# Projection, attention and state-update kernel: where three bonus-related steps stand, narrower turned rows, and another order of the sample value products

## The reference, cut to what matters

```python
h = rmsnorm(x, norm_mix_g);  p = h @ w_in          # 1024 -> 2560 columns
pa, pb = p[..., :SHIFT_W], p[..., SHIFT_W:]        # group A (RWKV-7) and group B (attention)
# group A: token shift, per-head recurrence, bonus
xm = pa + mu_shift * (pa_prev - pa)                # pa_prev: the row before; for a sample, state_shift
bonus = sum(rh * kh * r_k, axis=-1, keepdims=True) * vh
# group B: sliding window of 128, 8 query heads on 2 kv heads, learned sinks, ALiBi
o = einsum('bkgts,bskd->btkgd', p, vals)           # sample: 128 cached rows + 4 new ones
x = x + concat(o_A, rmsnorm(o_B)) @ w_out
x = x + hier_moe(rmsnorm(x));  y = rmsnorm_final(x)
```

## Time and profile before

| | us |
|---|---|
| median of 3 executions | 1196.08 (1192.57 to 1202.50) |
| the profiled execution | 1196.84 |
| its span | 1195.0 |
| granted TensorE clock, mean of the span | 0.982 |

### The profile page before, as it was taken

How to read it: one execution, slowest core, us unless ns; L and a number is a source line. 1 busy time by engine, 2 the same in 40 slices (tenths; PEclk the granted TensorE clock), 3 DMA queues, 4 the chain that set the end, 5 groups by cost and what they waited for, 6 DMA issues and landing times.

```text
span 1195.0 us, 24875 instructions
## 1 busy us (share of the span) xinstructions
PE 1121.5 (94%) x10856; PEld 784.8 (66%) x10856; DVE 464.3 (39%) x930; ACT 362.8 (30%) x808; POOL 259.8 (22%) x153
## 2 busy tenths in 40 slices
PE   5999999999999978888899999889999999999995
PEld 4666666655566657677654444478778887888774
DVE  3300656537775586676835422441101000111034
ACT  3101645442435255654621311210111111011152
POOL 0000000001100059999910000111202112111102
PEclk9999989999999999989999999989999999999998
DMA  6511100001010130002041661268889889998894
GB/s 202 158 36 36 58 18 19 18 18 40 22 35 22 15 57 4 5 4 57 4 170 52 226 236 71 93 222 307 277 312 322 309 288 321 323 320 296 298 388 172
DMA packets 95689, 174.16 MB, mean 146 GB/s; under 512 B 19988, under 2 KB 41175, under 8 KB 95172
## 3 DMA queue, kind: packets, MB, share of 16 engines
q1 hardware_dynamic: 88372, 151.92, 36.6%
q0 software_dynamic: 7200, 20.57, 6.5%
HBM read 147.45 MB, written 27.75 MB: 147 GB/s over the span
## 4 chain that ended last, share of the span: by engine, by line
PE 85%; DVE 9%; issue 2%; ACT 2%; SPq 0%; DMA 0%; POOLq 0%; POOL 0%; DVEq 0%; ACTq 0%
PE ps L740 23%; PE ps L1446 20%; PE ps L1244 9%; PE ps L1469 9%; PE ps L1475 1%; PE ps L819 1%; PE ps L843 1%; PE ps L832 1%; PE ps L956 1%; PE ps L1422 1%; PE ps L997 1%; PE ps L944 1%; PE ps L1122 1%; ACT arena L1983 1%; PE ps L778 1%
## 5 line engine op out<-in xcount | busy, mean ns | idle before, releaser
L740 PE MATMUL ps<-arena 128*128 128x355 f32 x960 | 302.6, 472 | 1.9 <-issue 1.7
L740 PEld LDWEIGHTS ps<-arena 128*128 128x128 f32 x960 | 182.1, 193 | 109.2 <-issue 13.3
L1446 PEld LDWEIGHTS ps<-arena 128*128 128x128 f32 x2048 | 245.9, 191 | 7.8 <-issue 6.1
L1446 PE MATMUL ps<-arena 128*128 128x128 f32 (+4 forms) x2048 | 248.3, 283 | 0.7 <-ACT arena L1958 0.6
L1244 PE MATMUL ps<-arena 128*128 128x512 f32 x256 | 116.4, 597 | 0.7 <-DVE arena L2346 0.7
L1469 PE MATMUL ps<-arena 128*128 128x512 f32 x256 | 113.3, 595 | 0.7 <-DVE arena L2621 0.7
L1966 ACT ACTIVATE arena<-ps 128x128 f32<-128x128 f32 (+4 forms) x64 | 18.3, 286 | 278.5 <-PE ps L1446 278.5
L2621 DVE TENSOR_TENSOR arena<-arena,ps 128x128 f32<-128x128 f32 (+4 forms) x64 | 19.1, 298 | 212.6 <-ACT arena L1966 212.6
L2806 POOL TENSOR_TENSOR arena<-arena 128x1024 f32<-128x1024 f32 x4 | 11.4, 2853 | 334.5 <-DVE arena L2147 334.5
L1469 PEld LDWEIGHTS ps<-arena 128*128 128x128 f32 x256 | 47.4, 190 | 55.1 <-issue 53.6
L1555 ACT COPY arena<-ps 128x355 f32<-128x355 f32 x60 | 27.1, 452 | 184.8 <-PE ps L740 184.8
(11 more groups left out here) (416 smaller groups left out, 1558.5 us busy)
## 6 DMA issues: line engine op xcount, KB each, us to landing
arena<-in_w_exp_gate SPq DMA_DIRECT2D x16, 2048.0 KB, 10.8
arena<-in_w_exp_up SPq DMA_DIRECT2D x16, 2048.0 KB, 16.4
arena<-in_w_exp_down SPq DMA_DIRECT2D x16, 2048.0 KB, 15.3
arena<-in_w_in SPq DMA_DIRECT2D x16, 512.0 KB, 3.8
arena<-in_x_prompt SPq DMA_DIRECT2D x9, 512.0 KB, 4.4
x_dram<-arena SPq DMA_DIRECT2D x9, 512.0 KB, 3.6
h_dram<-arena SPq DMA_DIRECT2D x8, 512.0 KB, 2.6
out_y_prompt<-arena SPq DMA_DIRECT2D x8, 512.0 KB, 3.7
```

The costliest lines, as they stand in the source:

```text
L740: last = pe.matmul(ps[:, q % 2, 0:m], wr[:, n % 3, k, :], hT[:, k, a:a + m], start=(k == 0), stop=(k == KB - 1))
L1446: last = pe.matmul(ps[:, 3 + f % 2, n * CAP:n * CAP + CAPS[e]], w[a][:, k, f * P:(f + 1) * P], xgT[:, a, k, 0:CAPS[e]], start=(k == 0), st ...
```

## The change

- `hT` loses the gap columns: 1057 columns (`HW`), thirds of 353, 352 and 352 (`G3`). GpSimd's second memset goes. The sample tile is scaled like the others, with one instruction for each four feature blocks. `pT` keeps its gaps, so the third `evict` of each block becomes two copies: 320 prompt columns, and 32 sample columns spread over 8 groups of 4.
- `BONUS_AT` is 74, 86, 99, 117: `bonus`, `smp_turn` and `smp_copy` of the first two pairs stand one half later.
- `a_store(7)` stands before `evict(31)` instead of behind it.
- `s_out` makes both products with new rows first, and then alternates between the kv heads, sample by sample. The number of products stays.

```diff
+HW = 1 + TOK
-G3 = [(0, 355), (355, 355), (710, 355)]
+G3 = [(0, 353), (353, 352), (705, 352)]
...
-        hTf = part(HT0, KB * W)
+        hTf = part(HT0, KB * HW)
...
-        LORA_AT, KK_AT, BONUS_AT = ([2 * q + 1 for q in at] for at in ((31, 37, 43, 50), (33, 39, 45, 52), (36, 42, 49, 58)))
+        LORA_AT, KK_AT = ([2 * q + 1 for q in at] for at in ((31, 37, 43, 50), (33, 39, 45, 52)))
+        BONUS_AT = [74, 86, 99, 117]
...
-            return ap[:, :, 1 + SEQ:W].rearrange("p b (q t) -> p b q t", t=DT + 1)[:, :, :, 1:]
+            return ap[:, :, 1 + SEQ:1 + TOK]
...
-                for kv in range(BKV):
-                    r = slice(kv * HD, (kv + 1) * HD)
-                    out = ps[r, 7, 0:P]
-                    pe.matmul(out, kvnew[:, P + kv * HD:P + (kv + 1) * HD], spk1[:, kv * P:(kv + 1) * P], start=True, stop=False, skip_group_check=True)
-                    for b in range(DB):
-                        view = lambda ap: ap.rearrange("p (g b t) -> p g b t", g=GRP, b=DB)[:, :, b, :]
-                        last = pe.matmul(view(out), vc[:, b, r], view(spk0[:, kv * P:(kv + 1) * P]), start=False, stop=(b == DB - 1), skip_group_check=True)
+                half = [slice(kv * HD, (kv + 1) * HD) for kv in range(BKV)]
+                for kv, r in enumerate(half):
+                    pe.matmul(ps[r, 7, 0:P], kvnew[:, P + kv * HD:P + (kv + 1) * HD], spk1[:, kv * P:(kv + 1) * P], start=True, stop=False, skip_group_check=True)
+                for b in range(DB):
+                    view = lambda ap: ap.rearrange("p (g b t) -> p g b t", g=GRP, b=DB)[:, :, b, :]
+                    for kv, r in enumerate(half):
+                        last = pe.matmul(view(ps[r, 7, 0:P]), vc[:, b, r], view(spk0[:, kv * P:(kv + 1) * P]), start=False, stop=(b == DB - 1), skip_group_check=True)
...
-                act.copy(pT[:, pos, a:a + m], ps[:, q % 2, 0:m]).then_inc(s["p_ok"], 1)
+                if g < 2:
+                    act.copy(pT[:, pos, a:a + m], ps[:, q % 2, 0:m]).then_inc(s["p_ok"], 1)
+                else:
+                    act.copy(pT[:, pos, a:1 + SEQ], ps[:, q % 2, 0:m - NS])
+                    act.copy(sample4(pT[:, pos, 1 + SEQ:W]), by4(ps[:, q % 2, m - NS:m])).then_inc(s["p_ok"], 1)
...
-                if k >= 5 and k % 2:
+                if k >= 5 and k % 2 and k < NU + 3:
                     a_store((k - 5) // 2)
...
+                if UNIT_AT.get(h) == NU + 3:
+                    a_store(NT - 1)
                 if h % 2:
                     evict(h // 2)
...
-                    if t < NT:
-                        dve.tensor_tensor(dst, src, g[:, :, None].to_broadcast([P, 4, n]), ALU.mult).then_inc(s["hT_ok"], 1)
-                    else:
-                        for k in range(4):
-                            last = dve.tensor_scalar(dst[:, k], src[:, k].rearrange("p (b t) -> p b t", t=DT), g[:, k:k + 1], None, ALU.mult)
-                        last.then_inc(s["hT_ok"], 1)
+                    dve.tensor_tensor(dst, src, g[:, :, None].to_broadcast([P, 4, n]), ALU.mult).then_inc(s["hT_ok"], 1)
...
-            pool.memset(hT[:, :, 0:1], 0.0)
-            pool.memset(hT[:, :, 1 + SEQ:W:DT + 1], 0.0).then_inc(s["level_ok"], 1)
+            pool.memset(hT[:, :, 0:1], 0.0).then_inc(s["level_ok"], 1)
```

## The result

The changed kernel took 1187.0 us (median of 13, from 1181.2), the kernel before beside it 1193.3. The ratio is 0.9921, with a 95% interval of 0.9899 to 0.9943; one of the 13 executions of the changed kernel ran slow, at 3545.84 us, and isn't in it. The ratio is not that of the two medians, which stand only 6.3 us apart (0.9947); 0.9921 is 9.4 us. The forecast was 1186.8, within 1%. In a later comparison the changed kernel came to 0.9918 (0.9889 to 0.9947) and 1185.1 us.

The account below looks back on a forecast made before the run. TensorE, busy 94% of the span, was taken to bound the kernel. 2.1 + 6.0 + 1.2 + 0.9 - 0.2 = 10.0 us, from the profiled 1196.84, gave 1186.8 us (chance 0.50); range 1179 to 1194.

Parts of the forecast that it names:

- columns: Projection: thirds lose 2, 3 and 3 columns, so TensorE streams 2560 fewer; 2.1 us gained, bounds 0 and 2.2.
- bonus sums, second pair: Second bonus sum, one half later: its 2.04 us wait for DVE goes and the following step shortens by 0.1 us.
- bonus sums, first pair, with its fall: First bonus sum, one half later: 2.04 us wait and 1.95 us of clock fall go, 0.2 us new wait.
- attention copy: Before the first `lora`: with `a_store(7)` earlier, TensorE's wait goes; 1.2 us gained, bounds 1.0 and 1.3.
- value products: `s_out`: alternating kv heads lets weight loads overlap in the column halves; 0.9 us gained, bounds 0 and 1.3.
- fall behind `s_out`: Rival, more gain: a shorter `s_out` may remove the clock fall behind it, 1.7 us; around 1183 us, chance 0.28.
- split of the last copy: End of the projection: `r_turn` waits for the last third copy, now two instructions; 0.2 us lost.
- start, to `shift_turn`: Start of the projection: 0.07 us saved by five halves of the first third is lost in waiting for turned rows.
- later stages: After the projection: start earlier by the sum and keep their length, within 2 us.
- What bounds the kernel: Whole kernel: TensorE, busy 94% of the span; a change is worth what it takes from TensorE.
- what came late next: Before `lora(1)`, behind the moved first bonus sum: a new wait of 0.2 us for L2157.
- the forecast's own signs: Prediction wrong if the projection doesn't end 9 to 11 us earlier, or later stages' length changes beyond 2 us.

Follow-up runs that it names:

- rows as before: Changed kernel with the turned rows of before (1065 columns, thirds of 355, one copy for each third): 1185.2 us, ratio 0.9925.
- start filled: Changed kernel plus five products of 256 columns on constant data between and behind the first transposes, results overwritten: 1184.0 us, ratio 0.9908.
- store as before: Changed kernel with the last attention store behind the copy of half 63 again: one execution, 1191.2 us, no ratio.
- old order put back: Changed kernel with all value products of the first kv head before those of the second in `s_out`: 1187.8 us, ratio 0.9936.
- sums put back: Changed kernel with the first two bonus sums one half earlier, as before the change: 1189.8 us, ratio 0.9964.
- value products alone: Kernel before with only the alternating value products of `s_out`: 1193.1 us, ratio 0.9979.
- The repeat: The changed kernel itself, unaltered, measured and profiled a second time: 1185.1 us, profile span 1183.4.
- bonus sums alone: Kernel before with only the new places of the first two bonus sums: 1190.7 us, ratio 0.9962.

## Why the prediction was right, point by point

The table sets each term of the sum against sections of the traces between two fixed steps of TensorE. Except in the row of the first bonus pair, a fall of the clock in a section stands in its own row.

| term | forecast | measured | from |
|---|---|---|---|
| columns | 2.1 | 1.7 behind `shift_turn` | `shift_turn` to `r_turn`, no fall in either: 336.89 with the rows as before, 335.21 with the start filled |
| bonus sums, second pair | 2.15 | 2.4 | kk1 to `lora(2)`: 26.07 before, 23.67 after |
| bonus sums, first pair, with its fall | 3.8 | 3.7 | kk0 to `lora(1)`: 27.75, 24.01 |
| attention copy | 1.2 | 1.2 to 1.3 | the wait before; store as before |
| value products | 0.9 | 1.4 | old order put back |
| fall behind `s_out` | a rival | 1.7 | 4.28 - 2.56 |
| fall behind the first scores | not seen | 1.7 | 9.59 - 7.88 between the two score steps |
| split of the last copy | -0.2 | 0.0 | last bonus to `r_turn`: 8.26, 8.28 |
| start, to `shift_turn` | 0.07 lost | 0.95 gained | 64.73, 63.78 |
| later stages | 0 | -3.7 | windows above |
| sum | 10.0 | 11.0 | 1195.0 - 1184.0 |

Each of the two bonus rows also holds 0.08 us of the columns' gain (26.07 before, 25.99 with narrow rows and the sums put back), which the row of the columns has too; with that the rows add up to 11.1.

*What bounds the kernel.* Right: all that was won was won on TensorE, and of the work added on ACT only 0.06 us was seen, in the wait before `r_turn` (0.54, then 0.60).

*Columns.* Right in mechanism and size. The sections behind `shift_turn` hold 104 of the 120 halves, 1.9 us by the forecast's arithmetic, and 1.7 were measured. About 0.1 of the missing 0.2 went into the wait before `lora(1)`, where DVE sets the pace: from the first sum to it the narrow rows take 5.63 us and the wide ones 5.54. The first 16 halves should give the remaining 0.3; `shift_turn` starts at 61.98 to 65.59 in the ten profiles, so that part is not shown. The forecast's "five halves of the first third" at the start are four, 0.05 us in place of 0.07.

*Bonus sums.* Right, down to the price of what came late next: 0.2 us forecast before `lora(1)`, 0.3 measured. The wait of the second pair was computed as none and is none. The half that was put before the sum fills the wait, and nothing else behind it is late. The one risky term, the fall behind the first wait, was charged fully. Of the three profiles with that first wait two show it (kernel before, value products alone) and one doesn't (bonus sums put back); behind the second wait none of the three does. Of the seven profiles in which the sum was moved none has a fall there. Without any fall the two pairs gain 2.0 and 2.3 us (25.99 and 26.00 from kk to the next `lora` with the sums put back, 24.01 and 23.67 in the changed kernel), 4.3 together.

*Value products.* Right in mechanism, too low by 0.5. The step that was mis-sized is the choice between the bounds 0 and 1.3: loads that alternate between the column halves run fully side by side, 33 ns a record in place of 65. Here the measurement decides between the two pages of the Trainium skill that the forecast weighed. It goes against TensorE: Matmul & The Clock Gate ("The mechanism" of its Part 3), by which a load runs beside matmuls in flight only where the row group differs, and it agrees with TensorEngine Tiling (Array Packing), "Key Properties", by which different tiles load and multiply in parallel.

*The split copy.* Charged 0.2 and cost nothing in sum, as the 0.06 before `r_turn` were made up by `r_left`, which starts 4.45 us behind it (4.51 before): `r_left` waited for DVE (0.73 us by its row after, 0.80 before), and the copies on ACT were not what it waited for last.

*The later stages.* Here the forecast's sentence that they "keep their length" was wrong for this pair of profiles, and "If `s_out` is shorter, the fall behind it may go too", held for a rival, was what happened, though the old order put back didn't bring that fall again. By the forecast's own signs it failed twice: the stage was to end 9 to 11 us earlier and ended 14.7 earlier, and the later stages were to keep their length within 2 us and took 3.7 more. The two misses nearly cancel: 3.4 us of falls and 0.95 at the start that went in the projection, 3.7 lost later. That the total of the profiles came out right is partly luck. So is the agreement of 1186.8 with 1187.0: the forecast started from an execution of 1196.84 us, and the median of 13 was 1193.3. The repeat shows how little of this belongs to the kernel: the same code had a recurrence of 198.6 and of 197.1 us. Over all ten profiles, whose recurrence is the same code, it took 196.2 to 202.5 us, and the kernel before happened to be profiled at the shortest. So the 3.7 are, as far as the runs show, the scatter of the executions and no price of the change. Which share of that scatter is the clock is open. Time at the lower clock alone doesn't order the lengths: four profiles with 10.2 us of the recurrence at 1.2 GHz took 196.2, 198.0, 198.5 and 198.7 us, two with 17.1 us took 198.6 and 202.5.

The better anchor is the sum of what doesn't depend on the clock: 1.7 for the columns (with 0.3 at the start by arithmetic 2.0), 4.3 for the bonus sums, 1.2 and 1.4, together 8.9 us, and some share of the falls. The ratio's interval is 6.8 to 12.1 us of 1193.3, and 8.9 lies inside it.

The single edits don't contradict it: bonus sums alone 0.9962, value products alone 0.9979, which from the 1195.4 beside them are 4.5 and 2.5 us, for 4.3 and 1.4 by the sections; the intervals are wider than these differences, and that of the value products includes no gain.

## What to carry to other kernels

Cut the trace into sections between fixed steps of the bounding engine and compare these, not the totals: 0.40 us of narrower products was visible in one section of 53 us, while the total with and without them could not be told apart. And count how often a fall of the clock comes in several profiles before its going is put down to an edit. When a step waits for another engine, count how long that engine needs from its last input and put just as much independent work before the step; then check what stands behind it, as here the next consumer was 0.3 us late. Small products that use one half of the array are worth reordering so that neighbours use different halves, 1.4 us here.

## What the runs showed of the hardware that I had not expected

The clock falls are not fixed to places in the program. Behind the first sample scores it fell in five profiles of ten (kernel before, bonus sums back, old value products, bonus sums alone, value products alone) and not in the other five; behind the second it fell in six. Of six stands of 2.04 or 2.11 us before a bonus sum it fell behind two. In the projection, where TensorE is back to back, each fall cost 1.7 us. Two of the ten profiles have none there (rows as before, start filled), the kernel before has four.

Weight loads for the two column halves of the array run side by side: 32 records in 1.04 us when they alternate, 16 in as much when they don't.

At the start, the first half of the projection took 2.61 to 5.07 us in the ten profiles. Whether products with a thrown-away result, put in TensorE's waits there, make it short each time is open: the one profile with them has 2.61, one without them 2.63.
